# First expert gathers interleaved with the query projections on PE, ScalarE and GpSimd

## What is computed

```
for each token x (after rms_norm with ffn_norm), 8 heads:
  q = x @ w_query                                   # 8 heads x 2 halves x 128
  sc = q . sub_keys                                 # 128 scores per half
  top_s, top_i = top_k(sc, 16)                      # per half
  best_s, pos  = top_k(sums of the 16 x 16 pairs, 16)
  experts = row numbers among 16384;  gates = softmax(best_s)
  act = gelu(expert_down[experts] . x)              # 16 dots of length 1024
  y  += sum_k (gates * act)_k * expert_up[experts]_k
```

## Time and profile before

| | us |
|---|---|
| median of 3 runs | 1511.02 (1509.93 to 1512.76) |
| the profiled execution: its time | 1507.68 |
| the profiled execution: its span in the trace | 1505.9 |
| PE busy | 1260.8 (84%) |
| VectorE busy | 802.2 (53%) |
| ScalarE busy | 597.7 (40%) |
| GpSimd busy | 889.2 (59%) |
| gathers' DMA queue | 268.45 MB, 43.0% of 16 engines' span |
| stream's DMA queue | 123.35 MB, 25.9% |

### The profile page before, as it was taken

How to read it: one execution, slowest core, us unless ns; L and a number is a source line. 1 busy time by engine, 2 the same in 40 slices (tenths; PEclk the granted TensorE clock), 3 DMA queues, 4 the chain that set the end, 5 groups by cost and what they waited for, 6 DMA issues and landing times.

```text
span 1505.9 us, 17590 instructions
## 1 busy us (share of the span) xinstructions
PE 1260.8 (84%) x5876; PEld 896.8 (60%) x5876; DVE 802.2 (53%) x1544; ACT 597.7 (40%) x1247; POOL 889.2 (59%) x541
## 2 busy tenths in 40 slices
PE   6878887867778887777777777899999979799998
PEld 5667766833333333333333333689999958699886
DVE  6763434387776666677777744332453642346401
ACT  5445543343222333333332322346555334455432
POOL 6773475764444445544444441496868854689985
PEclk9999898988999898999989999999999999899999
DMA  7343344899999999999999997364645633455563
GB/s 248 125 139 106 119 126 159 331 366 420 419 420 421 419 421 420 420 420 420 420 420 415 421 420 308 100 198 141 180 133 175 221 108 112 126 159 185 189 189 104
DMA packets 72945, 400.70 MB, mean 266 GB/s; under 512 B 8097, under 2 KB 8353, under 8 KB 39713
## 3 DMA queue, kind: packets, MB, share of 16 engines
q0 software_dynamic: 36864, 268.45, 43.0%
q1 hardware_dynamic: 33696, 123.35, 25.9%
q10 hardware_dynamic: 2304, 7.85, 1.5%
HBM read 396.48 MB, written 3.15 MB: 265 GB/s over the span
## 4 chain that ended last, share of the span: by engine, by line
PE 28%; issue 20%; DMA 17%; POOL 16%; DVE 15%; ACT 2%; POOLq 0%; ACTq 0%; DVEq 0%
DMA arena<-in_experts,arena 15%; POOL w_lo L1114 14%; PE bank L683 8%; PE bank L506 6%; PE bank L507 6%; PE bank L508 6%; DMA late_rows<-in_experts,arena 2%; DVE arena L1360 1%; DVE arena L1364 1%; DVE arena L1362 1%; DVE arena L1414 1%; POOL stat L1088 1%; DVE arena L1363 1%; ACT arena L971 1%; DVE arena L1359 1%
## 5 line engine op out<-in xcount | busy, mean ns | idle before, releaser
L1114 POOL TENSOR_TENSOR w_lo<-ring,w_hi 128x1024 fp32r<-128x1024 f32 x224 | 565.2, 2541 | 197.9 <-ACT w_hi L833 197.0
L683 PE MATMUL bank<-arena,diag 128*128 128x512 f32 x872 | 426.2, 647 | 127.4 <-ACT diag L977 127.3
L1157 POOL DMA_INDIRECT arena<-in_experts,arena x218 | 246.7, 1132 | 283.5 <-PE bank L683 238.5
L683 PEld LDWEIGHTS bank<-arena,diag 128*128 128x128 f32 x872 | 177.9, 208 | 373.4 <-issue 224.0
L1414 DVE CUSTOM_DVE_ANT_0 arena<-arena 128x1024 f32<-128x1024 f32 x218 | 262.1, 1225 | 156.0 <-DMA arena<-in_experts,arena 156.0
L833 ACT ACTIVATE w_hi<-ring 128x1024 fp32r<-128x1024 f32 x228 | 240.3, 1059 | 231.1 <-PE bank L508 192.3
L506 PE MATMUL bank<-hT_hi,w_hi 128*128 128x256 f32 x864 | 250.2, 290 | 15.3 <-POOL w_lo L1114 7.9
L507 PE MATMUL bank<-hT_lo,w_hi 128*128 128x256 f32 x864 | 248.1, 287 | 0.0
L508 PE MATMUL bank<-hT_hi,w_lo 128*128 128x256 f32 x864 | 247.9, 287 | 0.0
L968 ACT ACTIVATE arena<-arena 128x4 f32<-128x4 f32 x64 | 13.1, 205 | 437.8 <-DVE arena L1414 437.7
L506 PEld LDWEIGHTS bank<-hT_hi,w_hi 128*128 128x128 f32 x864 | 169.9, 197 | 17.2 <-issue 10.5
(11 more groups left out here) (211 smaller groups left out, 1569.6 us busy)
## 6 DMA issues: line engine op xcount, KB each, us to landing
ring<-in_stream SPq DMA_DIRECT2D x228, 512.0 KB, 3.5
arena<-in_experts,arena POOLq DMA_INDIRECT x218, 18.4
kv_park<-arena ACTq DMA_DIRECT2D x8, 256.0 KB, 4.1
arena<-kv_park ACTq DMA_DIRECT2D x1, 2048.0 KB, 7.6
x_res<-in_x SPq DMA_DIRECT2D x2, 512.0 KB, 5.4
arena<-in_mem SPq DMA_DIRECT2D x1, 1024.0 KB, 11.4
arena<-in_sub_keys ACTq DMA_DIRECT2D x1, 1024.0 KB, 5.0
out<-arena SPq DMA_DIRECT2D x2, 512.0 KB, 2.6
```

Of the source, the lines that this page charges most:

```text
L683: mm = pe.matmul(y_banks[half][:, :], diag[:, slot % DIAGS, :], rows_buf[slot % GATHERS][:, D + 512 * half:D + 512 * half + 512], start=(i ...
L1114: nc.gpsimd.tensor_tensor(w_lo[:, slot, :], ring[:, slot, :], w_hi[:, slot, :].bitcast(F32), ALU.subtract).then_inc(S("lo_made"), 1)
L1157: nc.gpsimd.indirect_dma_start(out=rows_buf[b], out_offset=None, in_=experts, in_offset=bass.IndirectOffsetOnAxis(ap=expert_u[:, slot:slot ...
```

## The change

- The order of the query stage is QUERY_ORDER: query 0, scores 0, query 1, and then query h, scores h - 1 for h = 2 to 7, and scores 7.
- Before scores 5 PE, and ScalarE with the two first gate_exps, do slots 0 to 3; before query 7 slots 4 to 7; before scores 6 slots 8 to 11. The others follow behind scores 7, on ScalarE behind hi_parts and gate_exps(2).
- GpSimd makes low parts to query chunk 5, gathers 0 and 1, and then one low part before each of gathers 2 to 8 (chunks 6 to 12); chunks 13 to 15 before gather 9; the next four before gather 18.
- Slots 0 to 17 use nine row buffers in turn, so gathers 9 to 17 wait for slots 0 to 8. The ninth buffer is where queryT had its heads 4 to 7; queryT now holds two heads, and ScalarE waits for scores h - 2 before it copies query h. From slot 18 on all 13 buffers are in turn; gathers 18 to 21 are the first in the other four and wait for scores 7.
- The sub-keys and gain rows are asked for before ScalarE's part of the ffn norm.
- The y results are opened in the plan before scores 5 (tile 0) and behind scores 7 (tile 1), and are signalled by a semaphore of their own, y_done. VectorE's order is unchanged.

```diff
 BATCH = 4
 GATHERS = 13
 DIAGS = 8
-FIRST_LO = 10
-FIRST_GATHERS = 8
+EARLY = 9
+EARLY_SLOTS = 12
+LO_FIRST = 6
+BUFFER = [s % EARLY if s < 2 * EARLY else (s - EARLY) % GATHERS for s in range(SLOTS)]
+USES = [BUFFER[:s + 1].count(BUFFER[s]) for s in range(SLOTS)]
+EARLIER = [max((i for i in range(s) if BUFFER[i] == BUFFER[s]), default=None) for s in range(SLOTS)]
 STREAM = [("w_in", 24), ("xk", 8), ("xv", 8), ("w_out", 8), ("query", 16),
           ("in_nat", 20), ("in_sqk", 8), ("in_conv", 12), ("in_gate", 24), ("branch", 12), ("w_o", 8),
...
 for _name in ("ffn", "xa", "mlp", "final"):
     HALVES[_name] = [(0, 0), (0, 1), (1, 0), (1, 1)]
 NORMS = ["attn", "mem", "ffn", "mix", "xa", "mlp", "final"]
+QUERY_ORDER = [("query", 0), ("sub", 0), ("query", 1)]
+for _h in range(2, PEER_H):
+    QUERY_ORDER += [("query", _h), ("sub", _h - 1)]
+QUERY_ORDER.append(("sub", PEER_H - 1))
+STEP_SLOTS = {QUERY_ORDER.index(_key): range(4 * _i, 4 * _i + 4)
+              for _i, _key in enumerate([("sub", PEER_H - 3), ("query", PEER_H - 1), ("sub", PEER_H - 2)])}
+FIRST_STEP = min(STEP_SLOTS)
 def plan():
...
         add(("mixT", g))
     natural("w_out", 2, 4, FIRST["w_out"])
     norm("ffn")
-    for h in range(PEER_H + 1):
-        if h < PEER_H:
-            add(("query", h), FIRST["query"] + 2 * h + 1)
-        if h > 0:
-            add(("sub", h - 1))
-    for t in range(TT):
-        for half in range(2):
-            add(("y", t, half))
+    for step, (kind, h) in enumerate(QUERY_ORDER):
+        if step == FIRST_STEP:
+            for half in range(2):
+                add(("y", 0, half))
+        add((kind, h), FIRST["query"] + 2 * h + 1 if kind == "query" else None)
+    for half in range(2):
+        add(("y", 1, half))
     norm("mix")
     natural("in_nat", 5, 4, FIRST["in_nat"])
     transposed("in_sqk", 4, FIRST["in_sqk"])
...
-        queryT = A(4096, 4096).rearrange("p (h w t) -> p h w t", h=8, w=2)
+        queryT = A(4096, 1024).rearrange("p (h w t) -> p h w t", h=2, w=2)
...
-        rows_buf = [A(16384 + 2048 * i, 2048) for i in range(8)] + [A(4096 + 2048 * i, 2048) for i in range(3)] \
+        rows_buf = [A(16384 + 2048 * i, 2048) for i in range(8)] + [A(6144, 2048), A(4096, 2048), A(8192, 2048)] \
             + [late_rows[:, 2048 * i:2048 * i + 2048] for i in range(2)]
         assert len(rows_buf) == GATHERS
...
             n_tile = PEER_H * PEER_K
             if slot % n_tile == n_tile - 1:
-                eng.wait_ge(result_done, at[("y", slot // n_tile, 1)][2])
+                eng.wait_ge(S("y_done"), 2 * (slot // n_tile) + 2)
             else:
                 eng.wait_ge(S("slot_used"), slot - slot // n_tile + 1)
...
                 for t in range(TT):
                     for w in range(2):
                         i = 2 * t + w
-                        mm = pe.matmul(bank[:, i * P:(i + 1) * P], queryT[:, h, w, t * P:(t + 1) * P],
+                        mm = pe.matmul(bank[:, i * P:(i + 1) * P], queryT[:, h % 2, w, t * P:(t + 1) * P],
                                        subk[:, 2 * h + w, :], start=True, stop=True)
                 mm.then_inc(result_done, 1)
-            for h in range(PEER_H + 1):
-                if h < PEER_H:
-                    transposed("query", h, normed("ffn") if h == 0 else None)
-                if h > 0:
-                    sub_scores(h - 1)
-            for t in range(TT):
-                y_banks = [open_bank(pe, ("y", t, half)) for half in range(2)]
-                n_tile = PEER_H * PEER_K
-                for i in range(n_tile):
-                    slot = t * n_tile + i
+            y_banks = {}
+            def add_slots(slots):
+                for slot in slots:
+                    t, i = divmod(slot, PEER_H * PEER_K)
+                    if i == 0:
+                        y_banks[t] = [open_bank(pe, ("y", t, half)) for half in range(2)]
+                    last = i == PEER_H * PEER_K - 1
                     pe.wait_ge(S("diag_made"), slot + 1)
                     for half in range(2):
-                        mm = pe.matmul(y_banks[half][:, :], diag[:, slot % DIAGS, :],
-                                       rows_buf[slot % GATHERS][:, D + 512 * half:D + 512 * half + 512],
-                                       start=(i == 0), stop=(i == n_tile - 1))
-                        if i == n_tile - 1:
-                            mm.then_inc(result_done, 1)
-                    if i < n_tile - 1:
+                        mm = pe.matmul(y_banks[t][half][:, :], diag[:, slot % DIAGS, :],
+                                       rows_buf[BUFFER[slot]][:, D + 512 * half:D + 512 * half + 512],
+                                       start=(i == 0), stop=last)
+                        if last:
+                            mm.then_inc(S("y_done"), 1)
+                    if not last:
                         mm.then_inc(S("slot_used"), 1)
+            for step, (kind, h) in enumerate(QUERY_ORDER):
+                if step in STEP_SLOTS:
+                    add_slots(STEP_SLOTS[step])
+                if kind == "query":
+                    transposed("query", h, normed("ffn") if h == 0 else None)
+                else:
+                    sub_scores(h)
+            add_slots(range(EARLY_SLOTS, SLOTS))
             norm("mix", xn)
...
                 split_hi(("mixT", g), [hT[k] for k in ks], [ghead[:, k:k + 1] for k in ks])
-            sumsq("ffn", xs, xn)
-            norm_out("ffn", con("g_ffn"))
             act.wait_ge(S("kv_parked"), 16 * 8)
             act.dma_start(subk, sub_keys).then_inc(S("subk_loaded"), 16)
             act.dma_start(gain_rows, ffn_rows).then_inc(S("gain_loaded"), 16)
-            for h in range(PEER_H + 1):
-                if h < PEER_H:
-                    copy_out(("query", h), queryT[:, h, :, :])
-                if h > 0:
-                    copy_out(("sub", h - 1), scores[:, h - 1, :, :, :])
-            hi_parts(LAST["query"] + RING)
+            sumsq("ffn", xs, xn)
+            norm_out("ffn", con("g_ffn"))
             def gate_exps(u):
...
                     nc.scalar.activation(diag[:, i % DIAGS, :], ident, ACT.Copy,
                                          scale=w_slot[:, i % 16:i % 16 + 1]).then_inc(S("diag_made"), 1)
-            for u in range(UNITS):
-                if u == 0:
-                    for first in range(2):
-                        gate_exps(first)
-                for b in range(PEER_K // BATCH):
-                    weigh(u * PEER_K + b * BATCH)
-                    if b == 2 and u + 2 < UNITS:
-                        gate_exps(u + 2)
-                    if u == PEER_H and b == 3:
-                        sumsq("mix", xs, xn, (0,))
+            for step, (kind, h) in enumerate(QUERY_ORDER):
+                if step in STEP_SLOTS:
+                    if step == FIRST_STEP:
+                        for first in range(2):
+                            gate_exps(first)
+                    weigh(STEP_SLOTS[step][0])
+                if kind == "query":
+                    if h >= 2:
+                        wait_evacuated(act, ("sub", h - 2))
+                    copy_out(("query", h), queryT[:, h % 2, :, :])
+                else:
+                    copy_out(("sub", h), scores[:, h, :, :, :])
+            hi_parts(LAST["query"] + RING)
+            gate_exps(2)
+            for slot in range(EARLY_SLOTS, SLOTS, BATCH):
+                u, b = slot // PEER_K, slot % PEER_K // BATCH
+                weigh(slot)
+                if b == 2 and u + 2 < UNITS:
+                    gate_exps(u + 2)
+                if u == PEER_H and b == 3:
+                    sumsq("mix", xs, xn, (0,))
             sumsq("mix", xs, xn, (1,))
             for a, first, w in c3_parts:
                 act.dma_start(A(a, w), c3_in[:, first:first + w]).then_inc(S("c3_loaded"), 16)
...
             rsqrt(o_rs[:, 0:16], o_ss[:, 0:16], 1.0 / 64, S("att_rstd"))
             rsqrt(o_rs[:, 16:24], o_ss[:, 16:24], 1.0 / 128, S("att_rstd"))
             norm("ffn")
-            lo_parts(FIRST["query"] + FIRST_LO - 1)
+            lo_parts(FIRST["query"] + LO_FIRST - 1)
             def gather(slot):
-                u, b = slot // PEER_K, slot % GATHERS
+                u, b = slot // PEER_K, BUFFER[slot]
                 pool.wait_ge(S("experts_ready"), u + 1)
-                if slot >= GATHERS:
-                    used_by(pool, slot - GATHERS)
-                elif slot >= 8:
+                if EARLIER[slot] is not None:
+                    used_by(pool, EARLIER[slot])
+                elif slot >= 2 * EARLY:
                     wait_evacuated(pool, ("sub", PEER_H - 1))
                 nc.gpsimd.indirect_dma_start(
                     out=rows_buf[b], out_offset=None, in_=experts,
...
                   .then_inc(S(f"rows_landed{b}"), 16)
             for slot in range(SLOTS):
-                if slot == FIRST_GATHERS:
+                if 2 <= slot < EARLY:
```

(14 more changed lines are left out.)

## The result

The changed kernel takes 1523.55 us in the median of 5 runs (1520.32 to 1527.08), beside 1511.02 for the kernel before (5 runs, 1507.99 to 1513.61). The ratio is **1.0086, with a 95% interval of 1.0069 to 1.0103**: slower by 12.5 us, where I had forecast 6.9. The profiled execution took 1526.31 us with a span of 1524.5, against 1507.68 and 1505.9.

A forecast was written before the change was run, and what follows sets the result against it. The prediction took the issue of the early gathers, then back-to-back DMA transfers at 420 GB/s, as the bound. Its terms put gather 18 at 340.1 against 333.2, +6.9 us on the median of 1511.02: 1517.9, range 1512 to 1525.

The forecast's parts named there:

- The ramp: The moment from which the DMA never runs dry, and gathers issued by then; measured at gather 18, old 333.2, new 340.1.
- the two stretches of low traffic: DMA below 300 GB/s near 295 to 304 and 326 to 341 us, in place of one hole near 300.
- Start of the queries: PE starts query 0 at 236.05 us, not 240.66, 4.6 earlier, with sub-keys asked for some 30 us earlier.
- Head 0: Scores of head 0 made right behind query 0: selection starts 9.4 us earlier, gather 0 at 256.0, 12.7 earlier.
- Queries and gathers interleaved: A low part and gather take 3.43 us, chunk 16's load 8.5; gather 8 at 281.5, dots at 292.9.
- Slots 0 to 11: Gelu to gather takes 6.20 us for slot 0, 4.34 for slot 4; gather 9 at 303.8, gather 17 at 329.7.
- The last term ahead of gather 18: On GpSimd four low parts, 9.35 us, stand between gather 17 at 329.7 and gather 18 at 340.1.
- The full stretch: Behind gather 18, 238 transfers of 2.50 us at 420 GB/s follow in either kernel, so no difference.
- Rival 1: Even: same mechanism with the low bounds, +0.9 to +3 us, 1512 to 1514; chance 0.16.
- Rival 2: Faster: transfers, not issues, set the ramp; DMA full from gather 9 on, -6.9 us, 1504.1; chance 0.15.
- Rival 3: Slower still: ring loads and gathers hinder each other more, two loads at 11.6 not 8.5, 1524.1 us; chance 0.08.
- Rival 4: Query 0 did not wait for the sub-keys: start stays at 240.66, all 4.6 later, 1522.5 us; chance 0.03.

The follow-up runs named there:

- b_keys_early: The kernel before with only the wait on the parked keys and the sub-key DMAs moved ahead of the ffn norm: 1509.00 us, ratio 0.998.
- a_keys_late: The changed kernel with the sub-keys and gain rows asked for behind the ffn norm again: 1526.87 us, ratio 1.0113.
- a_lo_late: The changed kernel with low parts 16 to 19 ahead of gather 25 instead of gather 18: 1523.79 us, ratio 1.0082.
- n_no_slots: The changed kernel with slots and gate exponentials behind all queries, 13 buffers from the start, low parts 16 to 19 ahead of gather 9: 1506.72 us, ratio 0.9969.
- b_head0: The kernel before with sub-keys early and head 0 scored right behind query 0, no interleaved low parts, no ninth early buffer: 1506.57 us, ratio 0.9977.
- a_gates_early: The changed kernel with the two first gate exponentials ahead of query 6's copy on ScalarE: 1519.69 us, ratio 1.0048.
- n_gates_early: n_no_slots with the two first gate exponentials ahead of query 6's copy: 1509.35 us, ratio 0.9988.
- n_lo7: n_no_slots with one more low part, query chunk 6, ahead of gather 0: 1506.90 us, ratio 0.9972.

## Why the prediction was right in sign and range, and short in size

The ramp was the right measure: the gathers' issue up to number 18 sets the end, slots on PE set the gathers, and the two stretches of low traffic stand where they were named (143 GB/s, then 309 and 290). The measured 1523.55 lies in the range. The sum of +6.9 was too small by 5.6, of which 4.0 is up to gather 18:

- **Start of the queries.** Right: 1.96 against 1.75, and b_keys_early and a_keys_late move it alone by 4.4 and 4.6.
- **Head 0.** Gather 0 came at 22.8 and not 21.7: 1.1 too small, 0.2 of it from the start. PE was at 1.2 GHz for the first 5.3 us of query 0; in the old kernel it was for 3.4. I had kept the old duration.
- **Queries and gathers interleaved.** A pair of one low part and one gather took 3.55 us and not 3.43: 0.8 by gather 8. Selection 1 grew beside the low parts by more than the 4 us foreseen, from 9.6 us for selection 0 to 20.2 (one pair of operations took 3.43 us, 0.76 when alone), and was hidden all the same: VectorE idled 15.12 us behind it. The load of chunk 16 took 9.7 us from the end of low part 12, not the 8.5 that I had picked between 3.5 and 11.6. By the gate exponentials 0.9 of this is left, and the dots behind them gave back 0.2. The Trainium skill, "DMA: Bandwidth & Descriptors", section "Queues, rings and completion order", has the engines take queues in turn; by that the load would have been about 6, so here the measurement stands against the estimate made from it.
- **Slots 0 to 11.** Gelu to gather 9 took 6.20, as forecast to the hundredth, and 4.32 for slot 4. For slot 8 it took 4.97, not 4.34, with a mean granted clock of 0.65 in its last 3 us (1.00 for slot 4): +0.6. The turn between the first two groups was 0.2 shorter.
- **The last term ahead of gather 18.** The four low parts took 10.26 and not 9.35, low part 19 having waited 0.97 for its high part, which stands behind the scores of head 7: +1.0. a_lo_late shows that this term had a second one under it. "9.35 us of low parts" was no price of theirs: without them the same scores hold gather 18, and 3.5 is all they cost.
- **The full stretch.** I had set its rate equal. From gather 18 to the last dot it took 607.2 us, against 605.6 from the place that I had given gather 18 in the old sequence: +1.6. Most of it is in this one row, which at 420 GB/s would have taken 2.0 us less; the old kernel's lowest such row, 411, costs 0.4.

```profile
840.00:860.00 20.00, 17.13 (x40) 7.19 (x39) 11.88 (x32) 4.67 (x18) 11.51 (x11) 1.00 0.94 379
```

Such a stretch near 820 to 860 is in other kernels too (411 GB/s before, 379 in n_no_slots, 384 in b_head0), and the last two are faster than before, so I hold this term for one that varies and not for the change's; that is not shown. Its cause stays open.

**The rivals.** Rival 1 falls: it wanted several terms at their low bounds, and five terms (head 0, the pairs, the load, slot 8, the low parts) lay above what I took; two of them, the pairs and the low parts, stood in no bound of mine. Rival 2 falls: from gather 9 on the DMA was not full, and gather 18 decided, at +10.9. Rival 3 has part of the truth, the load of 9.7, but n_no_slots has the same loads beside the same gathers and is faster than before. Rival 4 falls at b_keys_early.

What I didn't ask is where the parts stood to each other. The change is two good steps and one bad: sub-keys early gains 2.1 us in the old kernel and 3.3 in the new, head 0 at once some 2 (not clear of noise), interleaved low parts and gathers nothing, and slots with nine buffers in turn lose about 17. Without the last it is 1506.7 us, 0.3% faster than before; b_head0 gets there with a much smaller edit.

## What to carry to other kernels

Where the end is set by a stream of transfers, count the bytes that are behind it at the first moment after which both kernels run at full rate; the difference over that rate is the change in time, and here that accounts for ten kernels within 2 us. Fewer buffers taken sooner are worth it only if the work that frees them doesn't pass through several engines in turn: here each reuse went from dots over weights to a slot on PE, with query copies between, and starved the DMA twice. And before a piece is priced as what stands ahead of an event, look for what stands under it; two waits that overlap give back only the difference. Work moved into an idle stretch of one engine is not free if another engine slows it there: beside GpSimd's low parts this took 1.9 us from a_gates_early, and from n_gates_early and n_lo7 the whole gain that was expected.

## What was new about the hardware

- A dot of 128x1024 on VectorE takes 1.22 us alone and 3.35 to 3.46 beside GpSimd's low part; four low parts took 9.32 us alone and 13.00 with the dots beside them. Moving VectorE's work earlier into that stretch lost 2.6 us. A cast of 128x32 took 0.18 us alone and 2.33 beside a low part.
- PE's granted clock stayed at 1.2 GHz for 5.3 us of query 0, and for 3.4 us in the old kernel. Both had waited 5.2 us ahead of the 2 us of the norm's transposes; between these and query 0 the new kernel waited 0.7 us and the old one 5.11. In the new kernel the stretch from N + 60 to N + 80 has a mean granted clock of 0.69 and the two behind it 0.91 and 0.83, where PE waits between the groups of slots.
- A load of 0.5 MB that lands in 3.4 to 4.3 us ahead of the gathers took 8.3 to 9.6 from its issue beside a gather every 3.55 us.
